# Both score parts of a pair's first head ahead of the transposed units, in the attentions of groups three and four

## The chip, the cores and the metric

One core of a Trainium2 chip runs the whole program. The metric is device time in microseconds (us); of several runs the median is taken. Five engines matter: TensorE (PE in the rows; PEld is its weight load), VectorE (DVE), ScalarE (ACT), GpSimd (POOL) and the DMA queue of SyncE (SP). Each runs its own instructions in program order and waits on semaphores for the others.

## What is computed

One layer of a decoder block over 2048 rows of 1024 columns: a projection, a convolution branch and a sparse attention branch, a gated merge with an output projection, a feed-forward part, and norms. The change touches only the attention, cut here to what matters:

```python
def block(xs):                       # one block of 128 queries
    start, qb, qib, wb = xs
    ...
    _, idx = lax.top_k(score, topk)  # 256 keys of each query
    ...
    att = jnp.einsum('bqhd,bqkd->bhqk', qb, k_sel) * (HEAD_DIM ** -0.5)
    att = att - slopes[None, :, None, None] * dist[:, None]
    p = jax.nn.softmax(att, axis=-1)
    return jnp.einsum('bhqk,bqkd->bqhd', p, v_sel)   # 8 heads, one shared key and value
```

The kernel does not gather the 256 keys. It computes the scores of every key up to the query's own block, adds a mask M that holds the distance and shuts out the keys that were not picked, and takes the softmax over the whole row.

## The kernel before

The rows are worked on in four groups of 512 (g = 0 to 3 in the code, groups one to four here). A group passes through a projection phase, an attention phase "C" and a feed-forward phase; the phases of different groups follow each other on TensorE. `halved(g)` is true in groups three and four, where a query row has up to 1536 and 2048 keys.

An attention of a group has 16 **pairs** of heads, `i` = 0 to 15: four query blocks of 128 rows, in each four pairs. In a pair, `e` is 0 for the first head and 1 for the second. The row of scores of a head has two **parts** in groups three and four: the first of 1024 keys, the second of what is left, 128, 256, 384 and 512 keys in the four blocks of group three, and 640, 768, 896 and 1024 in those of group four. Four engines work on it:

- TensorE computes a part's scores (L2086, L2087: four matmuls of 512 columns, or two to four narrower ones) into one of two score banks, which alternate. A part waits until the part two before it has been masked (`s_masked`).
- VectorE masks a part (L1667: one operation that reads the bank, adds M, keeps the least value and writes `probs`; a short second instruction reads the accumulator). The second part of a head starts from the first one's least value, so it waits for it.
- ScalarE takes the exponential of a head in two instructions (L1028), one for the first half of the row's tiles and one for the second.
- TensorE transposes the probabilities of the **preceding** pair in **units** of two tiles and two heads (L2033, four matmuls of 128 columns) into banks 4 and 5, which alternate from unit to unit. ScalarE copies a unit out as its high part (L1048), VectorE then writes the low part (L1675), and TensorE multiplies both by the values (L2055, L2056) two units later. One matmul at L2063 spreads the reciprocal sums.

A unit waits for two things: the exponentials of its tiles (`exp_done`), and the low part of the unit two before it (`pt_ready`), whose bank it takes. The units of the preceding pair's first tiles (three in group three, four in group four) belong to `e` = 0, and those of its last tiles to `e` = 1. `woven(g, i, e, lag, at)` deals them out over the parts; TensorE (L2074) and VectorE (L1658) both walk its list, so that both have the same order:

```python
for v, ks in woven(g, i, e, lag, at):
    ...  # score part v (TensorE), or its mask (VectorE)
    for k in ks:
        transposes(k)
        values(k - 2)
```

ScalarE's own loop (L1039 on) goes by `at` and does not call `woven`: the high copies of a head's units, between them the second exponential of the head before, and then the first exponential of this head, once its last part is masked.

In what follows the first, second, third and fourth unit of `e` = 0 are called U0, U1, U2 and U3 (U3 stands in `e` = 1 in group three), and the first and second score part P0 and P1.

Of the kernel before, what the change touches and what calls it, by code (L numbers as in the profile page):

```python
# [23 lines left out]
def build_block(nc, A):  # L24
# [166 lines left out]
    with ctx:  # L191
# [160 lines left out]
        def woven(g, i, e, lag, at):  # L352

            n = parts_of(g) if i < PAIRS else 0
            ks = at[i - lag, e] if i >= lag else range(0)
            if n == 0:
                return [(None, ks)]
            cut = [len(ks) * v // n for v in range(n + 1)]
            return [(v, ks[cut[v]:cut[v + 1]]) for v in range(n)]

        PT_BASE = [sum(len(slots(a)[0]) for a in range(g)) for g in range(GROUPS)]

        def parts_of(g):

            return (g + 2) // 2
# [19 lines left out]
        def halved(g):  # L385

            return g >= 2
# [803 lines left out]
        def _(dve):  # L1191
# [144 lines left out]
            for ph, g in ORDER:  # L1336
# [284 lines left out]
                elif ph == "C":  # L1621
# [18 lines left out]
                    for i in range(PAIRS + lag):  # L1640
# [4 lines left out]
                        for e in range(2):  # L1645
# [12 lines left out]
                            for v, ks in woven(g, i, e, lag, at):  # L1658
                                if v is not None:
                                    s, w = part_span(b, v)  # L1660
                                    r = part(g, i, e, v)
                                    last = v + 1 == parts_of(g)
                                    dve.wait_ge(s_psum, r + 1)
                                    if v:
                                        dve.wait_ge(s_masked, r)
                                    out = top if last else first_top[:, e:e + 1]
                                    nc.vector.tensor_tensor_reduce(out=prob(g, i, e)[:, s:s + w], in0=score_bank(r)[:, 0:w],  # L1667
                                                                   in1=M[:, b % RT % 2, s:s + w].bitcast(f32), scale=-2.0 ** -(h + 1),
                                                                   scalar=low, op0=ALU.add, op1=ALU.min, accum_out=out).then_inc(s_masked, 1)
                                    low = out  # L1670
                                for k in ks:

                                    w = table[k][2] * 2 * P
                                    dve.wait_ge(pt_hi, PT_BASE[g] + k + 1)
                                    nc.vector.tensor_tensor(out=pt_hl(g, k, len(table), 1, w), in0=PS[:, 4 + k % 2, 0:w],  # L1675
                                                            in1=pt_hl(g, k, len(table), 0, w).bitcast(f32), op=ALU.subtract).then_inc(pt_ready, 1)
                                    if marking and step < MARKS:
                                        mark(t, RT * g + t, u_mark, step)
                                        step += 1
                                    weigh(k - 3)  # L1680
# [83 lines left out]
        def _(pe):  # L1764
# [116 lines left out]
            for ph, g in ORDER:  # L1881
# [132 lines left out]
                elif ph == "C":  # L2014
# [50 lines left out]
                    for i in range(PAIRS + lag):  # L2065
                        for e in range(2):
                            if i < PAIRS:
                                t, h = i // (HEADS // 2), 2 * (i % (HEADS // 2)) + e
                                if g > 0 and t == 0 and e == 0:
                                    pe.wait_ge(qs_in[h // 2] if h else qs_first, 16 * g)  # L2070
                                elif g > 0 and t == 1 and h == 0:
                                    pe.wait_ge(qs_in[0], 16 * g)
                                lhs = QS[:, h, t * P:(t + 1) * P]
                            for v, ks in woven(g, i, e, lag, at):  # L2074
                                if v is not None:
                                    r = part(g, i, e, v)
                                    s0, w0 = part_span(RT * g + t, v)
                                    if r >= PART_BASE[g] + 2:
                                        pe.wait_ge(s_masked, r - 1)
                                    elif g > 0:  # L2080

                                        pe.wait_ge(ny_done, RT * (g - 1) + r - PART_BASE[g] + 1)
                                    for at_s in range(0, w0, 512):
                                        s, w = s0 + at_s, min(512, w0 - at_s)
                                        o = score_bank(r)[:, at_s:at_s + w]
                                        mm(o, lhs, KH[:, s:s + w], start=True, stop=False)  # L2086
                                        ins = mm(o, lhs, KL[:, s:s + w], start=False, stop=True)  # L2087
                                    ins.then_inc(s_psum, 1)
# [3 lines that stand above are left out]
# [65 lines left out]
```

## Time and profile before

| | |
|---|---|
| runs | 3293.29 us median of three (3289.09 to 3296.37) |
| profiled execution, span | 3293.2 us |
| TensorE busy | 3180.6 us (97%) |
| VectorE, ScalarE, GpSimd busy | 2023.7 (61%), 1300.5 (39%), 790.1 us (24%) |
| attention of group three, 1795 to 1942 us | TensorE busy 130.65 of 147 us, VectorE 117.00, ScalarE 120.09 |
| attention of group four, 2656 to 2845 us | TensorE busy 174.44 of 189 us, VectorE 149.38, ScalarE 150.47 |

The span is the time from the first to the last instruction of one execution. A busy time is a sum over the engine's instructions. In the two attentions VectorE and ScalarE have four fifths of the time filled, against 61% and 39% over the whole program.

### The profile page before, as it was taken

The numbers are of one execution on the slowest core, as the hardware profiler recorded it, in microseconds if no ns is written. First come the engines' busy times: TensorE is split into PE (matmuls) and PEld (weight loads), VectorE is DVE, ScalarE is ACT, GpSimd is POOL, SyncE is SP. The second block draws the span as 40 slices with busy tenths as digits, with TensorE's granted clock in tenths as the row PEclk, the third lists the DMA queues.
The fourth block names the chain that finished last, engine by engine and source line by source line (L and its number), as shares of the span: only waits on it lengthen the run. The fifth ranks groups of instructions, "written<-read, shape, count | busy, mean of one in ns | idle before, by whom it ended". The sixth has DMA issues, their size and how long they took to land.

```text
span 3293.2 us, 41912 instructions
## 1 busy us (share of the span) xinstructions
PE 3180.6 (97%) x15077; PEld 2620.5 (80%) x15077; DVE 2023.7 (61%) x3433; ACT 1300.5 (39%) x2213; POOL 790.1 (24%) x674
## 2 busy tenths in 40 slices
PE   8987999999999999999999999999999999999998
PEld 7865788788888888778887878876888888788886
DVE  6997357688807447599895862759667588510001
ACT  4336421533237431351112854228675168420111
POOL 3432200065775100011313520000212325101212
PEclk9998999999999999999999999999999999999999
DMA  7973856599893656535555046552555520445554
GB/s 236 302 242 128 307 188 208 185 292 289 290 298 122 243 202 216 195 139 194 192 192 185 14 182 226 206 180 90 217 192 193 201 74 20 173 166 193 194 196 165
DMA packets 178529, 635.97 MB, mean 193 GB/s; under 512 B 11358, under 2 KB 96906, under 8 KB 116777
## 3 DMA queue, kind: packets, MB, share of 16 engines
q1 hardware_dynamic: 164016, 583.05, 51.0%
q10 hardware_dynamic: 14328, 50.42, 3.9%
q8 instruction: 121, 1.98, 0.2%
q14 instruction: 64, 0.52, 0.0%
HBM read 474.04 MB, written 159.38 MB: 192 GB/s over the span
## 4 chain that ended last, share of the span: by engine, by line
PE 78%; ACT 5%; issue 3%; DVE 3%; DMA 1%; POOL 0%; ACTq 0%; DVEq 0%; POOLq 0%; SPq 0%
PE PS L1862 19%; PE PS L1813 15%; PE PS L1815 15%; PE PS L1814 15%; PE PS L2033 3%; PE PS L1836 2%; PE PS L1837 1%; PE PS L1838 1%; ACT TMP L903 1%; PE PS L2055 1%; PE PS L2056 1%; ACT probs L1028 1%; DVE W L1405 1%; PE PS L2086 1%; PE PS L2087 1%
## 5 line engine op out<-in xcount | busy, mean ns | idle before, releaser
L1862 PE MATMUL PS<-WS,HT 128*128 128x512 f32 x2088 | 482.7, 391 | 3.3 <-POOL WS L571 3.3
L1862 PEld LDWEIGHTS PS<-WS,HT 128*128 128x128 f32 x2088 | 393.9, 189 | 85.8 <-issue 3.7
L704 POOL TENSOR_TENSOR TMP<-TMP 128x512 f32<-128x512 f32 x88 | 114.5, 1302 | 1294.6 <-ACT TMP L1153 1294.6
L571 POOL TENSOR_TENSOR WS<-RAW,WS 128x1024 fp32r<-128x1024 f32 x116 | 279.9, 2413 | 569.1 <-ACT WS L776 556.3
L1813 PE MATMUL PS<-HF,WS 128*128 128x512 f32 x1024 | 398.7, 389 | 1.3 <-ACT TMP L903 0.9
L1815 PE MATMUL PS<-HF,WS 128*128 128x512 f32 x1024 | 398.4, 389 | 0.0
L1814 PE MATMUL PS<-HF,WS 128*128 128x512 f32 x1024 | 398.4, 389 | 0.0
L1422 DVE TENSOR_SCALAR_CACHE_REDUCE flags<-W,cand 128x640 uint8<-128x640 f32 (+9 forms) x272 | 372.6, 1370 | 35.6 <-DVE cand L1457 27.8
L1813 PE MATMUL PS<-HT,WS 128*128 128x512 f32 x816 | 322.2, 395 | 0.3 <-DVE HT L1242 0.3
L1815 PE MATMUL PS<-HT,WS 128*128 128x512 f32 x816 | 317.8, 389 | 0.0
L1814 PE MATMUL PS<-HT,WS 128*128 128x512 f32 x816 | 317.5, 389 | 0.0
L776 ACT ACTIVATE WS<-RAW 128x1024 fp32r<-128x1024 f32 x114 | 120.7, 1059 | 329.7 <-PE PS L1815 118.5
L1753 DVE TENSOR_TENSOR attn<-PS,XR 128x1024 f32<-128x1024 f32 x16 | 19.1, 1220 | 364.5 <-PE PS L1862 364.1
L1322 DVE SCALAR_TENSOR_TENSOR PS<-W,cw,PS 128x512 f32<-128x512 f32 x344 | 227.2, 744 | 0.0
L1813 PEld LDWEIGHTS PS<-HF,WS 128*128 128x128 f32 x1024 | 192.2, 188 | 42.1 <-ACT TMP L903 1.3
L1814 PEld LDWEIGHTS PS<-HF,WS 128*128 128x128 f32 x1024 | 192.2, 188 | 40.0
L1815 PEld LDWEIGHTS PS<-HF,WS 128*128 128x128 f32 x1024 | 192.2, 188 | 39.9
L2033 PE MATMUL PS<-ident,probs 128*128 128x128 f32 x1088 | 173.0, 280 | 25.1 <-ACT probs L1028 15.4
L1862 PE MATMUL PS<-W,HT 128*128 128x512 f32 x792 | 185.2, 389 | 0.0
L903 ACT ACTIVATE TMP<-PS 128x512 f32<-128x512 f32 (+3 forms) x304 | 155.7, 546 | 67.0 <-PE PS L1913 44.7
L1813 PEld LDWEIGHTS PS<-HT,WS 128*128 128x128 f32 x816 | 153.2, 188 | 34.5 <-issue 2.5
L1814 PEld LDWEIGHTS PS<-HT,WS 128*128 128x128 f32 x816 | 153.2, 188 | 33.0 <-issue 1.9
(287 smaller groups left out, 6417.0 us busy)
## 6 DMA issues: line engine op xcount, KB each, us to landing
WS<-split_weights_scratch SPq DMA_DIRECT2D x234, 1024.0 KB, 4.8
split_weights_scratch<-WS SPq DMA_DIRECT2D x116, 1024.0 KB, 5.0
W<-split_weights_scratch SPq DMA_DIRECT2D x114, 1024.0 KB, 4.8
RAW<-in_w_in SPq DMA_DIRECT2D x34, 512.0 KB, 6.1
RAW<-in_w_ffn_gate SPq DMA_DIRECT2D x22, 512.0 KB, 6.3
RAW<-in_w_ffn_up SPq DMA_DIRECT2D x22, 512.0 KB, 6.4
RAW<-in_w_ffn_down SPq DMA_DIRECT2D x22, 512.0 KB, 5.7
gate_b_scratch<-TMP ACTq DMA_DIRECT2D x32, 256.0 KB, 5.3
```

Of the source, the lines that this page charges most:

```text
L571: nc.gpsimd.tensor_tensor(out=WS[:, slot, 1, :], in0=RAW[:, slot, :], in1=WS[:, slot, 0, :].bitcast(f32), op=ALU.subtract).then_inc(w_lo, 1)
L704: nc.gpsimd.tensor_tensor(out=TMP[:, s, :], in0=TMP[:, s, :], in1=TMP[:, 2 + s, :], op=ALU.mult).then_inc(h_prod, 1)
L776: nc.scalar.activation(WS[:, slot, 0, :], RAW[:, slot, :], ACT.Copy).then_inc(w_hi, 1)
L903: nc.scalar.activation(TMP[:, idx_done % 4, 0:w], PS[:, idx_bank(g, n), 0:w], ACT.Relu, scale=DH ** -0.5).then_inc(idx_relu, 1)
L1322: nc.vector.scalar_tensor_tensor(out=TAPSUM[:, c, :], in0=GLU[:, c, ds(k0 + i, ROWS)], scalar=cw[:, c, ds(k0 + i, 1)], in1=TAPSUM[:, c, :] ...
L1422: step(nc.vector.tensor_scalar(flags[:, 0:n], keys(g, t, 0, n), cand[:, t:t + 1].bitcast(f32), 0.0, op, ALU.add, accum_out=count[:, t:t + 1]))
L1813: mm(PS[:, bank, :], wh, src[:, 0, k, :], start=k == 0, stop=False)
L1814: mm(PS[:, bank, :], wh, src[:, 1, k, :], start=False, stop=False)
L1815: ins = mm(PS[:, bank, :], wl, src[:, 0, k, :], start=False, stop=k == KD - 1)
L1836: mm(o, split(c, 0)[:, at], src(0, k), start=k == 0, stop=False)
L1862: ins = mm(PS[:, 2 * t + half, :], lhs, split(c, w_part)[:, half * 512:(half + 1) * 512], start=first and part == 0 and w_part == 0, stop= ...
L2033: ins = nc.tensor.transpose(PS[:, 4 + k % 2, (2 * a + e) * P:(2 * a + e + 1) * P], prob(g, i, e)[:, (k0 + a) * P:(k0 + a + 1) * P], ident[ ...
```

## The change

Where a group is halved, all units that belong to a pair's first head come behind its second part. Before, they were dealt out over both parts: in group three one unit behind P0 and two behind P1, in group four two and two. The second head keeps its order, and so do groups one and two, which have one part a head.

```diff
@@ -356,6 +356,8 @@
             if n == 0:
                 return [(None, ks)]
             cut = [len(ks) * v // n for v in range(n + 1)]
+            if halved(g) and e == 0:
+                cut[1:n] = [0] * (n - 1)
             return [(v, ks[cut[v]:cut[v + 1]]) for v in range(n)]
```

TensorE in group three, first head of pair 10: P0 of 1024 keys, U0 with the values of an older unit, P1 of 384 keys, and U1. Before:

```order
L2086 MATMUL PS<-KH,QS 128x512 [waits scores_masked]
L2087 MATMUL PS<-KL,QS 128x512
L2086 MATMUL PS<-KH,QS 128x512
L2087 MATMUL PS<-KL,QS 128x512
L2033 MATMUL PS<-ident,probs 128x128 [waits pt_ready,exp_done]
L2033 MATMUL PS<-ident,probs 128x128 x3
L2055 MATMUL PS<-PT,VV 128x256 [waits pt_ready]
L2056 MATMUL PS<-PT,VV 128x256
L2055 MATMUL PS<-PT,VV 128x256
L2056 MATMUL PS<-PT,VV 128x256
L2086 MATMUL PS<-KH,QS 128x384 [waits scores_masked]
L2087 MATMUL PS<-KL,QS 128x384
```

With the change (every line number is two higher):

```order
L2088 MATMUL PS<-KH,QS 128x512 [waits scores_masked]
L2089 MATMUL PS<-KL,QS 128x512
L2088 MATMUL PS<-KH,QS 128x512
L2089 MATMUL PS<-KL,QS 128x512
L2088 MATMUL PS<-KH,QS 128x384 [waits scores_masked]
L2089 MATMUL PS<-KL,QS 128x384
L2035 MATMUL PS<-ident,probs 128x128 [waits pt_ready,exp_done]
L2035 MATMUL PS<-ident,probs 128x128 x3
L2057 MATMUL PS<-PT,VV 128x256 [waits pt_ready]
L2058 MATMUL PS<-PT,VV 128x256
L2057 MATMUL PS<-PT,VV 128x256
L2058 MATMUL PS<-PT,VV 128x256
```

The two matmuls of P1 have moved ahead of U0 and of the four value matmuls behind it.

VectorE in group four, first head of pair 15: the mask of P0 (it writes `first_top`), the low parts of units, and the mask of P1 of 1024 keys (it reads `first_top`). Before:

```order
L1667 ISA probs,first_top<-PS,QI 128x1024 [waits s_psum,pt_psum]
L1667 ISA first_top 128x1
L1675 TENSOR_TENSOR PT<-PS,PT 128x512 [waits pt_hi] x2
L1667 ISA probs,mx<-PS,QI,first_top 128x1024 [waits scores_masked,s_psum]
L1667 ISA mx 128x1
L1675 TENSOR_TENSOR W<-PS,W 128x512 [waits pt_hi] x2
L1694 RECIPROCAL rs<-rs 128x2 [waits sums_of_halves_added]
```

With the change:

```order
L1669 ISA probs,first_top<-PS,QI 128x1024 [waits s_psum,pt_psum]
L1669 ISA first_top 128x1
L1669 ISA probs,mx<-PS,QI,first_top 128x1024 [waits scores_masked,s_psum]
L1669 ISA mx 128x1
L1677 TENSOR_TENSOR PT<-PS,PT 128x512 [waits pt_hi] x2
L1677 TENSOR_TENSOR W<-PS,W 128x512 [waits pt_hi] x2
L1696 RECIPROCAL rs<-rs 128x2 [waits sums_of_halves_added]
```

The mask of P1 has moved ahead of the low parts of U0 and U1, and stands directly behind the mask of P0.

## Rows read from the trace of the kernel before

**Rows 1.** The page, part 4: the chain that ended last, by engine.

```profile
PE 78%; ACT 5%; issue 3%; DVE 3%; DMA 1%; POOL 0%; ACTq 0%; DVEq 0%; POOLq 0%; SPq 0%
```

**Rows 2.** Waits, total us, times, longest: 1795 to 1942 us, then 2656 to 2845.

```profile
PE PS L2033 <- ACT probs L1028: 8.8, 14, 1.1
...
PE PS L2033 <- ACT probs L1028: 6.6, 15, 1.3
```

**Rows 3.** Timeline, group four, pair 15, first head: start, duration, engine, operation, idle before.

```profile
2815.06 0.40 PE L2086 MATMUL PS<-KH,QS 128*128 128x512 f32 x1
...
2815.29 0.40 PE L2087 MATMUL PS<-KL,QS 128*128 128x512 f32 x1
...
2816.56 0.66 PE L2033 MATMUL PS<-ident,probs 128*128 128x128 f32 x4 [0.41 <-ACT probs L1028]
2816.97 0.36 PE L2055 MATMUL PS<-W,VV 128*128 128x256 f32 x1
...
2819.60 0.60 PE L2033 MATMUL PS<-ident,probs 128*128 128x128 f32 x4
2819.95 0.36 PE L2055 MATMUL PS<-PT,VV 128*128 128x256 f32 x1
2820.11 1.27 DVE L1667 CUSTOM_DVE_ANT_0 probs<-PS,QI,first_top 128x1024 f32<-128x1024 f32 x1
...
2821.31 0.69 DVE L1675 TENSOR_TENSOR W<-PS,W 128x512 fp32r<-128x512 f32 x1
```

**Rows 4.** Timeline, group three, pair 10, first head.

```profile
1873.68 0.40 PE L2086 MATMUL PS<-KH,QS 128*128 128x512 f32 x1
...
1874.76 0.66 PE L2033 MATMUL PS<-ident,probs 128*128 128x128 f32 x4
1874.92 1.23 DVE L1667 CUSTOM_DVE_ANT_0 probs<-PS,QI 128x1024 f32<-128x1024 f32 x1 [0.49 <-PE PS L2087]
...
1876.08 0.69 DVE L1675 TENSOR_TENSOR W<-PS,W 128x512 fp32r<-128x512 f32 x1
...
1876.97 0.60 PE L2033 MATMUL PS<-ident,probs 128*128 128x128 f32 x4
```

**Rows 5.** Timeline, VectorE, group four, pair 0: masks of P0 and P1.

```profile
2656.28 1.21 DVE L1667 CUSTOM_DVE_ANT_0 probs<-PS,QI 128x1024 f32<-128x1024 f32 x1
...
2657.64 0.88 DVE L1667 CUSTOM_DVE_ANT_0 probs<-PS,QI,first_top 128x640 f32<-128x640 f32 x1
```

**Rows 6.** Groups by form, group four, then group three: busy us, mean ns, idle.

```profile
L1667 DVE CUSTOM_DVE_ANT_0 probs<-PS,QI,first_top 128x1024 f32<-128x1024 f32 x8 | 10.2, 1275 | 0.0
...
L1667 DVE CUSTOM_DVE_ANT_0 probs<-PS,QI,first_top 128x128 f32<-128x128 f32 x8 | 2.8, 344 | 0.3
```

**Rows 7.** Timeline, group three, pair 2, first head.

```profile
1808.20 0.40 PE L2086 MATMUL PS<-KH,QS 128*128 128x512 f32 x1
...
1809.82 0.66 PE L2033 MATMUL PS<-ident,probs 128*128 128x128 f32 x4 [0.54 <-ACT probs L1028]
...
1811.14 0.69 DVE L1675 TENSOR_TENSOR PT<-PS,PT 128x512 fp32r<-128x512 f32 x1 [0.49 <-ACT PT L1048]
...
1811.98 0.41 PE L2033 MATMUL PS<-ident,probs 128*128 128x128 f32 x2
```

**Rows 8.** Timeline, group three, pair 6, first head: U0 and U2.

```profile
1841.46 0.66 PE L2033 MATMUL PS<-ident,probs 128*128 128x128 f32 x4 [0.78 <-ACT probs L1028]
...
1843.80 0.60 PE L2033 MATMUL PS<-ident,probs 128*128 128x128 f32 x4
```

**Rows 9.** Timeline, P0 and U2 of group three's last and group four's first such pair.

```profile
1917.10 0.40 PE L2086 MATMUL PS<-KH,QS 128*128 128x512 f32 x1
...
1920.96 0.60 PE L2033 MATMUL PS<-ident,probs 128*128 128x128 f32 x4
...
2672.27 0.40 PE L2086 MATMUL PS<-KH,QS 128*128 128x512 f32 x1
...
2676.07 0.62 PE L2033 MATMUL PS<-ident,probs 128*128 128x128 f32 x4
```

## Prediction

> **What bounds the kernel now.** I read the page's chain first, then the waits and the timeline of the two attentions. TensorE makes up 78% of the chain that ended last, ScalarE 5%, VectorE 3% [rows 1]: whatever makes TensorE wait inside an attention lengthens the program one for one, since the phases follow each other on TensorE. The waits tell what there is to win. TensorE's transposes stood still for ScalarE's exponential for 8.8 us in group three (14 times) and 6.6 us in group four (15 times) [rows 2], about once a pair. The timeline shows where: in pair 15 of group four TensorE has sent off P0 and sits idle 0.41 us until the exponential that U0 needs is done [rows 3]. The change puts P1 into this gap. What it takes away is VectorE's early turn at U0's low part.
>
> **The measure.** I count each pair from the start of its P0 to the start of U2. Behind U2 the order on all engines is the old one, so I take what follows to move with it. U2 has two conditions. TensorE must have reached it, and the low part of U0 must be written, since both use the same bank. Between the start of a low part and a unit that waited for it alone lie 0.84 us: pair 2 of group three, 1811.14 to 1811.98 [rows 7].
>
> **Where U2 is now.** The start of P0 to that of U2 is 1811.98 - 1808.20 = 3.78 us in pair 2 of group three and 1920.96 - 1917.10 = 3.86 in pair 15; 2676.07 - 2672.27 = 3.80 in pair 2 of group four and 2819.60 - 2815.06 = 4.54 in pair 15 [rows 3, 7, 9]. Read the same way, the 14 pairs from 2 to 15 give 3.78, 4.16, 4.17, 4.26, 4.22, 4.23, 4.32, 4.36, 3.29, 3.29, 3.40, 3.42, 3.87, 3.86 in group three, and 3.80, 3.81, 3.87, 3.97, 4.31, 4.33, 4.44, 4.44, 4.22, 4.23, 4.33, 4.46, 4.54, 4.54 in group four.
>
> **Where VectorE will be.** It masks P0 from 1.24 us behind the start of P0 on (1874.92 - 1873.68, [rows 4]). P1's mask needs P0's least value. The trace has the two masks back to back only in pair 0, where the second starts 2657.64 - 2656.28 = 1.36 us behind the first [rows 5]; I take that for all pairs. P1's mask holds VectorE for its duration less 0.07 us, since a 1.27 us mask at 2820.11 is followed by a low part at 2821.31 [rows 3]. By width that is 0.27 us for 128 keys and 1.20 for 1024 [rows 6], on a line between them 0.13 more for every 128 keys. So U0's low part starts no earlier than 1.24 + 1.36 + m, and U2 no earlier than 3.44 + m, with m the mask's step: 3.71, 3.84, 3.98 and 4.11 in the four blocks of group three, 4.25, 4.38, 4.51 and 4.64 in those of group four. Now the low part of U0 starts at 2.40 us in pair 10 (1876.08 - 1873.68 [rows 4]).
>
> The other bound on U0's low part is ScalarE's high part: it starts 1.32 us behind U0 (1811.14 - 1809.82 [rows 7]), hence U2 at U0 + 2.16. This holds only where U0 itself is late, in pairs 2 to 9 of group three, where ScalarE's exponentials come last.
>
> **The sum, pair by pair.**
> - Group three, pairs 2 to 5: U2 already stands at U0 + 2.16 (1811.98 - 1809.82 [rows 7]), and U0 waits for ScalarE whatever TensorE does. P1's mask fits in VectorE's idle time. 0.
> - Pairs 6 to 9: U2 stands at U0 + 2.34 (1843.80 - 1841.46 [rows 8]) in two of them and 2.45 in the other two, because P1 lies between; it can fall to 2.16. The gain is 0.18, 0.18, 0.29 and 0.30: -0.95.
> - Pairs 10 to 13: no wait for the exponential now (U0 at 1.08 [rows 4]), so P1's move covers nothing. U2 goes from 3.29, 3.29, 3.40, 3.42 to 3.98, 3.98, 4.11, 4.11: +2.8.
> - Pairs 14 and 15: 3.87, 3.86 to 4.11: +0.5.
> - Group four, pairs 2 to 5, 6 to 9, 10 to 13, 14 and 15: 4.25, 4.38, 4.51, 4.64 less the times above: +1.8, +0.3, +1.1, +0.2, together +3.4.
> - Pair 1 of each group: TensorE is not up to speed and the queues are still short; P1 ahead of U0 delays U0 by about 0.3 us in group three, and in group four fills a longer gap by as much. 0, give or take 0.5.
>
> That is +5.8 us. One term more: a unit behind a wait is slower at the start. In pair 15 the values follow 0.41 us behind U0, which waited, and 0.35 behind U2, which did not [rows 3]. U2 waits newly in 24 pairs: +1.3. The whole is **+7.1 us**, against the profiled execution's 3293.2 us 3300.3; the median of the runs, 3293.29, is the same time, so it stays **3300.3 us**.
>
> What I cost at nothing: P1's scores are the same matmuls, and their bank is free, since the part two before was masked before P0 began. U0 comes later by P1's length (0.12 to 0.93 us), less the wait that it fills. That delays U0's and U1's high parts on ScalarE; for U1's low part and so for the unit behind U2 it is about a tie in pairs 14 and 15 of group four, and if it isn't, each pair pays up to 0.3 us again. ScalarE's and GpSimd's loops and all DMA queues keep their order.
>
> **A rule weighed.** The step of 1.36 us between the masks holds a wait of VectorE on its own semaphore. Before a low part, which has no such wait, it is 1876.08 - 1874.92 = 1.16 us [rows 4], so the trace charges 0.20 for it. The Trainium skill, "VectorE: DVE Perf Modes", section on the DRAIN, says that a semaphore between VectorE operations costs nothing extra. By that rule the masks would follow each other at the plain step. This case's trace speaks against it in pair 0, with the 0.20 us just named.
>
> **The rivals.**
> 1. The forecast, VectorE's mask of P1 decides U2: +5.5 to +9 us. Chance 0.47.
> 2. Part of the delay is taken up again. In pairs 10 to 13 of group three TensorE has no gap, but if ScalarE or VectorE then sets the pace behind U2, the delay there costs half, 7.1 - 1.4 = 5.7, and with the same in the first block of group four, 5.7 - 0.9 = 4.8: +3 to +5.5 us, about 3297.5. For it: the two engines are busy 0.8 of the attention. Against: behind U2 the timeline shows hardly a stop of TensorE. Chance 0.20.
> 3. The masks follow each other at VectorE's plain step of 1.16 us. Then U2 is 0.20 us earlier in the 24 pairs that it decides, -4.8, and the total is +2.3 us, 3295.6. Against it is the only place that shows the step. Chance 0.15.
> 4. Faster: U0's low part is in time, and the filled gap is a gain. A part of 1024 keys takes four matmuls 0.23 us apart (2815.29 - 2815.06 [rows 3]), 0.93 us. In pair 15 of group four U0 would start behind two of them at 1.86 us instead of 1.50, and without P1 in between U2 would follow at 4.54 + 0.36 - 0.93, about 3.95, instead of 4.54, -0.6; some -0.5 in 14 pairs of group four and -0.2 in ten of group three: -9 us, 3284. It decides where U0's low part starts before about 3.05 us; the two masks alone end at 3.40 and more in group four. Chance 0.06.
> 5. Worse: U1's low part is late as well, because U0 is, and the unit behind U2 waits again. 0.3 us in 24 pairs on top: +14 us, 3307. For it the tie named above. Chance 0.12.
>
> **How the numbers follow.** A measurement of this kernel tells 0.2%, 6.6 us, from no change. The forecast sits at that edge: of its 0.47 I count 0.35 above it and 0.12 below. Slower by over 0.2%: 0.35 + 0.12 = 0.47. Within: 0.12 + 0.20 + 0.15 = 0.47. Faster: 0.06. The range reaches from 3291.5, which takes in rivals 2 and 3 with the runs' own spread of some 3 us, to 3307. The forecast's own range is 3298.8 to 3302.3.
>
> **What would show it.** In the changed trace TensorE's wait for the exponential should nearly vanish in group four and in the last blocks of group three, and a wait for VectorE's low part should stand before U2, some 0.5 to 0.9 us in the pairs of group four. The two masks should start 1.36 us apart in every first head. P0 to U2 should read 3.98 in pair 10 of group three and 4.64 in pair 15 of group four. The attention of group four should be 3 to 5 us longer, that of group three 2 to 4, and everything outside them unchanged. The prediction is wrong if the step between masks is 1.16, if U2 doesn't wait for VectorE, or if the part behind U2 gets shorter as U2 comes later.

## The result and the profile after the change

The changed kernel took 3302.68 us, the median of ten runs (3300.7 to 3304.85); the kernel before, on the same chip, 3294.64 us, also ten (3289.09 to 3297.58). The ratio is 1.0023, with a 95% interval of 1.0014 to 1.0032: slower by 7.6 us. (This ratio and those below are estimated from all runs; they are not the quotient of the two medians, which differ by 8.0 us here.) The forecast was 7.1 us slower.

The page of the changed kernel: its span, the busy times, and the chain that ended last.

```profile
span 3300.0 us, 41912 instructions
...
PE 3179.3 (96%) x15077; PEld 2623.3 (79%) x15077; DVE 2026.4 (61%) x3433; ACT 1300.3 (39%) x2213; POOL 795.5 (24%) x674
...
PE 76%; ACT 5%; DVE 5%; issue 3%; POOL 0%; DMA 0%; ACTq 0%; DVEq 0%; POOLq 0%; SPq 0%
```

The busy times are those of before to within 6 us on every engine: no work was added. In the chain TensorE lost two points and VectorE won two, against [rows 1]. The profiled execution took 3302.19 us, of which 3300.0 are the span, 6.8 more than before.

What TensorE's transposes waited for, in group three's attention (first three rows) and in group four's (last three): total us, times, longest.

```profile
PE PS L2035 <- ACT probs L1030: 6.0, 12, 1.1
...
PE PS L2035 <- DVE PT L1677: 3.0, 4, 0.9
PE PS L2035 <- DVE W L1677: 2.3, 4, 0.8
...
PE PS L2035 <- DVE PT L1677: 8.1, 14, 0.8
...
PE PS L2035 <- DVE W L1677: 2.4, 4, 0.7
PE PS L2035 <- ACT probs L1030: 2.4, 2, 1.3
```

Set beside [rows 2]: in group four the wait for the exponential fell from 6.6 to 2.4 us, and of its two cases one stands in pair 1 and the other behind the last head, so that none is left in pairs 2 to 15. In its place stand 10.5 us of waiting for VectorE's low parts (L1677), 9.6 of them before U2 in pairs 2 to 15. Before it was 1.0 us:

```profile
PE PS L2033 <- DVE PT L1675: 1.0, 4, 0.5
```

One wait was traded for a longer one.

The timeline of group three's pair 10, and behind the "..." that of group four's pair 15: start, duration, engine, operation, idle before.

```profile
1873.86 0.40 PE L2088 MATMUL PS<-KH,QS 128*128 128x512 f32 x1
...
1875.08 1.23 DVE L1669 CUSTOM_DVE_ANT_0 probs<-PS,QI 128x1024 f32<-128x1024 f32 x1 [0.46 <-PE PS L2089]
1875.12 0.60 PE L2035 MATMUL PS<-ident,probs 128*128 128x128 f32 x4
...
1876.46 0.62 DVE L1669 CUSTOM_DVE_ANT_0 probs<-PS,QI,first_top 128x384 f32<-128x384 f32 x1
...
1877.00 1.37 DVE L1677 TENSOR_TENSOR W<-PS,W 128x512 fp32r<-128x512 f32 x2
...
1877.83 0.63 PE L2035 MATMUL PS<-ident,probs 128*128 128x128 f32 x4 [0.73 <-DVE W L1677]
...
2821.77 0.39 PE L2088 MATMUL PS<-KH,QS 128*128 128x512 f32 x1
...
2822.99 1.23 DVE L1669 CUSTOM_DVE_ANT_0 probs<-PS,QI 128x1024 f32<-128x1024 f32 x1
...
2823.62 0.60 PE L2035 MATMUL PS<-ident,probs 128*128 128x128 f32 x4
...
2824.36 1.28 DVE L1669 CUSTOM_DVE_ANT_0 probs<-PS,QI,first_top 128x1024 f32<-128x1024 f32 x1
...
2825.57 0.69 DVE L1677 TENSOR_TENSOR PT<-PS,PT 128x512 fp32r<-128x512 f32 x1
...
2826.41 0.63 PE L2035 MATMUL PS<-ident,probs 128*128 128x128 f32 x4 [0.58 <-DVE PT L1677]
2826.50 0.69 DVE L1677 TENSOR_TENSOR PT<-PS,PT 128x512 fp32r<-128x512 f32 x1 [0.24 <-ACT PT L1050]
2826.79 0.36 PE L2057 MATMUL PS<-PT,VV 128*128 128x256 f32 x1
...
2827.35 0.62 PE L2035 MATMUL PS<-ident,probs 128*128 128x128 f32 x4
```

Read each part from the top: P0, its mask on VectorE, U0, the mask of P1, the low part of U0, and U2, which waited for it. In pair 15 U0 no longer waits (in [rows 3] it did, 0.41 us). U2 does: it stands 2826.41 - 2821.77 = 4.64 us behind P0, where it stood at 4.54. In pair 10 it is 1877.83 - 1873.86 = 3.97, and was 1876.97 - 1873.68 = 3.29 [rows 4]. The rows behind U2 in pair 15 show the next unit 0.94 us later, 0.85 behind the start of U1's low part at 2826.50.

Per attention I compare the stretch from the start of pair 2's P0 to the last matmul that spreads the sums (L2063 before, L2065 after). In group three it grew from 127.71 to 130.77 us, in group four from 167.18 to 170.87. Together that is 6.75 us of the span's 6.8.

### The profile page after: what moved, and what is told of

Its sections match the earlier page's. It is cut to its first block, busy times and chain, and to the rows that moved or that the text cites. A ratio compares the mean times of both kernels' runs of the same rounds, so it can differ in the third digit from the quotient of the medians.

```text
span 3300.0 us, 41912 instructions
## 1 busy us (share of the span) xinstructions
PE 3179.3 (96%) x15077; PEld 2623.3 (79%) x15077; DVE 2026.4 (61%) x3433; ACT 1300.3 (39%) x2213; POOL 795.5 (24%) x674
## 4 chain that ended last, share of the span: by engine, by line
PE 76%; ACT 5%; DVE 5%; issue 3%; POOL 0%; DMA 0%; ACTq 0%; DVEq 0%; POOLq 0%; SPq 0%
PE PS L1864 19%; PE PS L1815 15%; PE PS L1817 15%; PE PS L1816 15%; PE PS L2035 2%; DVE probs L1669 2%; PE PS L1838 1%; ACT TMP L905 1%; PE PS L1839 1%; PE PS L1840 1%; PE PS L2057 1%; PE PS L2058 1%; DVE W L1407 1%; PE PS L2088 1%; PE PS L2089 1%
## 5 line engine op out<-in xcount | busy, mean ns | idle before, releaser
L1864 PE MATMUL PS<-WS,HT 128*128 128x512 f32 x2088 | 481.8, 390 | 4.3 <-POOL WS L573 4.3
L1864 PEld LDWEIGHTS PS<-WS,HT 128*128 128x128 f32 x2088 | 392.9, 188 | 86.8 <-issue 5.1
L1864 PE MATMUL PS<-W,HT 128*128 128x512 f32 x792 | 185.2, 389 | 0.0
```

What stands on the lines that cost most here:

```text
L1864: ins = mm(PS[:, 2 * t + half, :], lhs, split(c, w_part)[:, half * 512:(half + 1) * 512], start=first and part == 0 and w_part == 0, stop= ...
```

## The experiments

The theory is the forecast's: in a first head VectorE now masks P1 before it writes U0's low part, and U2 waits for that. The rivals were that U1's low part or a late restart decides, that ScalarE paces the pair, or that TensorE's own order costs the time. Lengths of stretches are from pair 2's P0 to the last spread of sums, as above, each from one trace; the **period** of a pair is the time from its P0 to the next pair's. All medians are of 11 runs, but for the kernel with VectorE's order alone, with 4. Each is set against runs of the kernel before on the same chip. Where an interval reaches 1.0000 the time alone tells no difference, and the reading rests on the stretches.

**One group at a time.** The change in group three alone, and then in group four alone:

```diff
+            if g == 2 and e == 0:
+                cut[1:n] = [0] * (n - 1)
```
```diff
+            if g == 3 and e == 0:
+                cut[1:n] = [0] * (n - 1)
```

> The change in group three alone. If the cost is VectorE's mask of P1 ahead of U0's low part, pair by pair, the attention of group three is as in the changed kernel: P0 to U2 3.97 us in pair 10, the pairs 6 to 9 about 0.11 us shorter each, pairs 10 to 15 0.3 to 0.8 longer each, together +3.1 us, and the time is 3294.6 + 3.1 = 3297.7 us. The attention of group four keeps its old times, only 3 to 4 us later. If the loss were one of something that the two attentions share (a queue that stays late from one to the other), the two halves would not add up to the whole 8 us.

> The change in group four alone. VectorE's mask: the 14 pairs 2 to 15 are 0.07 to 0.56 us longer each, the first four and the fifth to the twelfth in turn as in the changed kernel, +3.7 us, with pair 1 some 0.5 us shorter: about 3297.8 us. Rival: the gain that the filled wait for the exponential promised shows here alone, some -5 us, 3290.

Measured: 3298.33 us against 3295.03 (ratio 1.0008, 0.9999 to 1.0017) and 3298.75 (1.0012, 1.0003 to 1.0021). In the traces the changed attention has the whole kernel's length to within 0.1 us, 130.70 in group three and 170.86 in group four, and the one left alone that of before, 127.68 and 167.18. The two costs add up, +3.0 and +3.7, and neither attention touches the other. The interval of the first kernel still takes in 1.

**One engine at a time.** `woven` got one more argument. In one kernel only TensorE passes `True`, so that VectorE keeps its old order; in the other only VectorE does.

```diff
-        def woven(g, i, e, lag, at):
+        def woven(g, i, e, lag, at, ahead):
...
+            if ahead and halved(g) and e == 0:
+                cut[1:n] = [0] * (n - 1)
```

> TensorE has the new order (P0, P1, then the units), VectorE the old one (the low parts of the first units ahead of P1's mask). My theory, that the loss is VectorE's order: U2 falls back to U0 + 2.16 us or to the time when TensorE reaches it: about 3.44 in pair 10 of group three (3.97 in the changed kernel), 3.56 in pairs 12 to 15, 4.0 in pair 15 of group four (4.64). The unit behind it, U3 in group four, then waits for U1's low part, because U0 came later by P1's length less the old wait: 0 to 0.25 us in each of 14 pairs. Sum about -1 in group three and +1.5 in group four: 3294 to 3297 us, 5 to 8 us below the changed kernel. Rival, that TensorE's own order costs: it stays near 3302 us. Rival, that only the wait for the exponential mattered: 3287 us or less.

> VectorE has the new order (both masks ahead of the low parts), TensorE the old one (P1 behind U0, in group four behind U0 and U1). My theory: U0's low part now waits for P1's scores and their mask. Group four: P1 is done 3.9 to 4.7 us behind P0's start, its mask 0.8 to 1.2 later, U2 0.84 behind that: +1.8 to +2.2 us in 14 pairs, +28. Group three: +0.3 to +0.8 in 14 pairs, +7. Together about 3329 us. If VectorE's order were harmless and TensorE's the cost, the time would be near 3294.6 us.

TensorE alone: 3295.41 us, ratio 1.0001 (0.9992 to 1.0010), and 126.59 and 167.07 us in the traces, -1.1 and -0.1. VectorE alone: 3335.53, ratio 1.0120 (1.0104 to 1.0135), and 135.23 and 197.80 us, +7.5 and +30.6; I had expected 3329. The waits of TensorE in this second kernel, in group four:

```profile
PE PS L2035 <- DVE PT L1677: 22.1, 13, 2.1
PE PS L2035 <- DVE W L1677: 7.0, 4, 1.8
PE PS L2035 <- ACT probs L1030: 6.6, 15, 1.3
```

The 6.6 us for the exponential are unchanged, and 29.1 us of waiting for VectorE stand beside them, where the kernel before had 1.0. This kernel loses more than the change does, because its mask of P1 also waits for scores that TensorE still sends behind the first units. The clean comparison is the changed kernel with TensorE's order alone: they differ in VectorE's order only, and it costs 4.2 us in group three and 3.8 in group four. TensorE's order by itself costs nothing. So the loss comes with VectorE's order. Why TensorE's alone gains so little in group four is in its timeline of pair 15:

```profile
2815.20 0.39 PE L2088 MATMUL PS<-KH,QS 128*128 128x512 f32 x1
...
2818.18 1.14 ACT L1030 ACTIVATE probs<-probs,mx 128x1024 f32<-128x1024 f32 x1
...
2819.15 0.63 PE L2035 MATMUL PS<-ident,probs 128*128 128x128 f32 x4
...
2819.31 0.59 ACT L1050 ACTIVATE PT<-PS 128x512 fp32r<-128x512 f32 x1
...
2819.94 0.69 DVE L1677 TENSOR_TENSOR PT<-PS,PT 128x512 fp32r<-128x512 f32 x1 [0.93 <-ACT PT L1050]
...
2820.77 0.63 PE L2035 MATMUL PS<-ident,probs 128*128 128x128 f32 x4 [0.53 <-DVE PT L1677]
```

U2 is early, 3.95 us behind P0 instead of 4.54. This is the value that the forecast's fourth rival gave for it. But the unit behind it waits for U1's low part, that one for its high part, and the high part stands on ScalarE behind an exponential of 1.14 us. It starts 5.57 us behind P0; before it was 5.45, 0.91 behind U2. The gain is gone one unit later.

**The chain between the masks cut.** The changed kernel, with P1's mask free of P0's least value. This leaves out part of the computation: the shift inside the softmax is then the least value of P1 and 0, not that of the whole row.

```diff
-                                    if v:
-                                        dve.wait_ge(s_masked, r)
...
-                                    low = out
+                                    low = 0.0
```

> The changed kernel, but P1's mask starts from the constant 0 instead of P0's least value and doesn't wait for P0's mask (so the shift of the softmax is the least of P1 and 0, not of the whole row; the output is another one). It measures the step between the two masks, which the forecast took as 1.36 us. My theory: 0.20 us of it is VectorE's wait on its own semaphore; the step falls to 1.16, P0 to U2 to 4.44 in pair 15 of group four, and 20 or more pairs are 0.20 us shorter: -4 to -5 us, 3298 us. By the Trainium skill, VectorE: DVE Perf Modes, on the DRAIN, the semaphore costs nothing extra and the step and the time stay at 1.36 and 3302.7 us.

Measured: 3295.29 us against 3294.37, ratio 1.0003 (0.9994 to 1.0012), and 128.17 and 167.28 us in the traces, 2.6 and 3.6 less than the changed kernel. I had expected 4 to 5 less in all. Pair 15 of group four, P0, VectorE and U2:

```profile
2811.47 0.40 PE L2086 MATMUL PS<-KH,QS 128*128 128x512 f32 x1
...
2812.70 1.22 DVE L1667 CUSTOM_DVE_ANT_0 probs<-PS,QI 128x1024 f32<-128x1024 f32 x1
...
2813.85 1.22 DVE L1667 CUSTOM_DVE_ANT_0 probs<-PS,QI 128x1024 f32<-128x1024 f32 x1
...
2815.00 0.69 DVE L1675 TENSOR_TENSOR PT<-PS,PT 128x512 fp32r<-128x512 f32 x1
...
2815.83 0.63 PE L2033 MATMUL PS<-ident,probs 128*128 128x128 f32 x4 [0.30 <-DVE PT L1675]
```

The step from mask to mask falls from 2824.36 - 2822.99 = 1.37 us to 1.15. P1's mask now holds VectorE 1.15 us instead of 2825.57 - 2824.36 = 1.21. Its start value is now a constant and no longer read from memory, as P0's always was, whose mask of the same width took 1.23 us where P1's took 1.28; this part I had not counted. Together 0.28 us a pair, and U2 moves by just that, from 4.64 to 2815.83 - 2811.47 = 4.36. In the 14 pairs of group four and in pairs 10 to 15 of group three it moves by 0.28 to 0.31, in pairs 8 and 9 of group three by 0.2, and in its pairs 2 to 7 by 0.1 or less. So VectorE's chain of masks decides U2 in 22 first heads, but not in the first ones of group three. The edit takes out the wait and the reading of the value together.

**ScalarE's order.** After the kernel with TensorE alone the exponential between the high parts was suspect. The second exponential of the head before is put behind the second high part instead of the first, in the kernel before and then with TensorE's new order:

```diff
-                                if u == 0:
+                                if u == (1 if halved(g) else 0):
                                     second_half(i, e)
```

> The kernel before, but ScalarE copies U1's high part ahead of the second exponential instead of behind it (groups three and four, both heads). U1's low part no longer waits for the exponential. In the kernel before U3 follows U2 by 0.92 us without a wait, so I expect next to nothing: 3293 to 3296 us. It is the partner of the next run.

> TensorE has the new order, VectorE the old one, and ScalarE copies U1's high part ahead of the second exponential. With TensorE's new order alone U3 stood still for U1's low part (1.62 us behind U2 instead of 0.92 in pair 15 of group four), which waits for that exponential. My theory: this is the second thing that eats the filled gap; with it gone U3 follows U2 by 0.95 us, and group four's 14 pairs are 0.1 to 0.55 us shorter than before, -5 us, group three's about -1: 3287 to 3291 us, and faster than both kernels. Rival: VectorE is then late with the second head's masks and the next pair's U0 waits again: 3293 to 3297 us.

Alone it gives 3299.74 us against 3294.37, ratio 1.0009 (1.0000 to 1.0018; its runs spread from 3292.95 to 3302.23, and the medians are 5.4 us apart), with 131.19 and 167.87 us in the traces: +3.5 in group three and +0.7 in group four, where I had expected nothing. U0 comes later there in pairs 6 to 9 (1.99 to 2.09 us behind P0 instead of 1.87 to 1.90), and the periods of pairs 10 to 14 grow by 0.25 to 0.5. With TensorE's new order it gives 3291.78 us, ratio 0.9994 (0.9985 to 1.0003), and 128.29 and 163.81: group four gains 3.4 us, group three loses 0.6. I had expected 3287 to 3291; by the time alone it is not told from the kernel before.

**What the pieces give together.** TensorE's order only in group three, but not in its third block; TensorE's order with the later exponential in the first heads of group four alone; and that same exponential in the changed kernel, whose VectorE has the new order:

```diff
+            if ahead and g == 2 and i // 4 != 2 and e == 0:
+                cut[1:n] = [0] * (n - 1)
```
```diff
-                                if u == 0:
+                                if u == (1 if g == 3 and e == 0 else 0):
```

> TensorE's new order in group three alone, without its third block (pairs 8 to 11), VectorE's order as before. Pairs 6 and 7 lose P1 between U0 and U2 (0.15 us each), pairs 14 and 15 gain about 0.3 each, pairs 12 and 13 lose 0.15 each: -0.5 us, no difference that can be measured; 3294 us.

> TensorE has the new order in both groups, VectorE the old one, and ScalarE copies U1's high part ahead of the second exponential only in first heads of group four. The run before this with the exponential late in both heads and both groups lost in group three (first exponentials later, U0 waits again) what it won in group four. My theory: group three now has the times of TensorE's new order alone (-1.1 us against the kernel before), and group four at least the gain of the later exponential, -3.4 us, likely -4 to -5 because the second heads get their exponential early again: 3289 to 3291 us. Rival: the second heads were not what held U0 up, and it stays at 3292 to 3293.

> The changed kernel, and ScalarE copies U1's high part ahead of the second exponential in first heads of group four. If VectorE's two masks are what holds U2, ScalarE's order can't help: P0 to U2 stays 4.64 us in pair 15 and the time stays 3301 to 3303 us. If the loss had come from U1's high part, it would fall to about 3298.

The first: 3297.37 us, ratio 1.0009 (1.0000 to 1.0018), though the stretch of group three is 0.75 us shorter and that of group four unchanged. In its trace pair 2 begins 2.6 us later than in that of the kernel before (1810.84 against 1808.20), of which more below. The second: 3292.88 against 3295.68, ratio 0.9989 (0.9980 to 0.9998), with 126.62 and 165.11 us, -1.1 and -2.1. It is the only kernel whose interval lies below 1, by 0.0002: a gain of some 0.1%, which the stretches bear out with 3.2 us. Its time is not in the 3289 to 3291 that I had expected but in what the rival gave, 3292 to 3293. The third: 3303.27, ratio 1.0019 (1.0010 to 1.0028), 130.71 and 171.01 us, as the change itself: while VectorE's masks decide U2, ScalarE's order is worth nothing.

The second kernel, first head of pair 14 of group four: P0, the high parts, the exponential, and the two units.

```profile
2800.74 0.39 PE L2088 MATMUL PS<-KH,QS 128*128 128x512 f32 x1
...
2804.14 0.60 ACT L1050 ACTIVATE PT<-PS 128x512 fp32r<-128x512 f32 x1 [0.31 <-PE PS L2035]
2804.63 1.14 ACT L1030 ACTIVATE probs<-probs,mx 128x1024 f32<-128x1024 f32 x1
2804.70 0.63 PE L2035 MATMUL PS<-ident,probs 128*128 128x128 f32 x4
...
2805.63 0.61 PE L2035 MATMUL PS<-ident,probs 128*128 128x128 f32 x4
```

U1's high part now stands ahead of the exponential, and the unit behind U2 follows it without a wait, 2805.63 - 2800.74 = 4.89 us behind P0, where TensorE's order alone had 5.57. Yet a pair's period is only 0.04 to 0.07 us shorter in pairs 9 to 14 than with TensorE's order alone, and 0.21 to 0.35 in pairs 2 to 8. In the last blocks the second heads gave back nearly all of it. The expected gain in group four, 4 to 5 us, came out as 2.1. The trace shows part of it: in the second heads of pairs 9 to 15 the last unit waits 0.21 to 0.31 us for the low part of the unit two before it, where with TensorE's order alone no second head of pairs 2 to 15 waits. The rest of the 0.5 to 0.6 us that these heads are longer I did not separate: with the exponential moved in both heads the periods of pairs 10 to 14 were 0.4 to 0.5 us shorter than here, and those of pairs 2 to 8 0.1 to 0.4 longer.

## Why the prediction was right

**The bound.** That what lengthens an attention lengthens the program one for one held: 6.75 us of attention, 6.8 of span, 7.6 of time. The median of 3302.68 us lies just above the forecast's own range, 3298.8 to 3302.3, because that range stood on 3293.29 for the kernel before, and ten runs gave 3294.64; the difference lies inside its +5.5 to +9.

**Where U2 stands.** The bound 3.44 + m was forecast as 4.25, 4.38, 4.51 and 4.64 us in the blocks of group four. Measured, the 14 pairs from 2 to 15: 4.24, 4.24, 4.40, 4.38, 4.38, 4.37, 4.54, 4.50, 4.51, 4.51, 4.66, 4.64, 4.64, 4.64. In pairs 10 to 15 of group three 3.98, 3.98 and four times 4.11 were forecast, and 3.97, 3.98, 4.15, 4.12, 4.12, 4.13 measured. The four terms are in the rows above: 1875.08 - 1873.86 = 1.22, 1876.46 - 1875.08 = 1.38, 1877.00 - 1876.46 = 0.54, 1877.83 - 1877.00 = 0.83.

**The sum.** U2's part was forecast at 5.8 us and came to 6.2, 2.8 in group three and 3.4 in group four. The difference is in pairs 6 to 9 of group three, whose gain was forecast at 0.95. U2 reached 4.07 and 4.08 in the first two, as it should, but 4.21 and 4.23 in the others instead of 4.03 and 4.06; the periods gained 0.44 in all. There VectorE decided already, where the forecast had ScalarE. In pair 8 it was still at an older low part when P0's scores were ready, so that its mask began 1.47 us behind P0 and not 1.24. The kernel before shows the same there, 1.46; the forecast had read the 1.24 in pair 10 and taken it for all pairs. The term for the slower restart was too large: forecast 1.3, and all that was lost behind U2 is 0.6. The values follow U2 by 2826.79 - 2826.41 = 0.38 us in pair 15 and by 0.39 in pair 10, against 0.35 unhindered, not by the 0.41 of a U0 that waited for ScalarE. Two terms were mis-sized, the first too low by 0.4 us and the second too high by 0.7. The mechanism was right; that the total came this near is partly luck. The stretches ahead of pair 2's P0, put at 0 give or take 0.5, came out 0.6 us longer in group three and 0.6 shorter in group four, which also cancels.

**The step of 1.36 between the masks.** It had one place in the trace to rest on, and it held: 1.37 and 1.38 in the two pairs shown, and U2 within 0.05 us of the bound 3.44 + m in each of the 20 pairs for which the forecast used it. (The third rival took 0.20 us off 24 pairs, -4.8; by the forecast's own sum it was these 20, -4.0.) The Trainium skill, "VectorE: DVE Perf Modes", section on the DRAIN, has a semaphore between VectorE operations cost nothing extra. By that rule the kernel with the chain cut should have kept its step; it fell to 1.15. So the third rival is out, and the measurement decides: what the page measured on copies does not hold here for an operation that waits for the one directly before and reads its result.

**The tie.** U1's low part was taken to be in time for the unit behind U2. In pair 15 it starts at 2826.50, and 0.84 us later is 2827.34; the unit stands at 2827.35, 0.94 behind U2, where an unhindered one stood 0.91 behind. A tie indeed, and the fifth rival is out for that reason alone: the cover was 0.03 us short, not 0.3.

**The rival that ended on the other side** was right in its sum for U2 (about 3.95; with VectorE's order kept 3.95), and wrong on two counts. With VectorE's new order U2 can't get there. And even there it brings next to nothing in group four, 0.1 us, since U1's low part is late by way of ScalarE. The prediction named that second stop for its own sum and in the fifth rival, but the fourth left it out: its 9 us would not have come even with U0's low part in time.

**What TensorE's order did.** The wait for the exponential vanished in group four as forecast, and in group three it stayed in pairs 2 to 9, where U0 waits for ScalarE whatever TensorE does.

## What to carry to other kernels

When an engine's gap is filled with work moved forward, look at who consumes that work, and what it now stands in front of there: here the gap was TensorE's, and the price was paid on VectorE, where P1's mask came ahead of an operation that frees a bank. A list that two engines share is worth splitting before it is changed, because the order that is good for the producer can be the wrong one for the consumer; TensorE's move without VectorE's cost nothing, and became a small gain only once ScalarE's order was made to fit as well. Follow a gain for at least two units past the wait that it removes: here U1's low part was nearly late already, and took the gain back.

## What the runs showed that was not expected

**A dependent operation on VectorE costs 0.2 us more.** With the wait for its predecessor's least value a mask starts 1.37 us behind it, without the wait and the value 1.15. The 0.22 us go with the wait and not with the reading as such: where P1's mask reads the value behind a low part, no idle time stands before it (0.0 us for the eight masks of 1024 keys in [rows 6]). With 0.06 us for each start value that is read, this made up 6.2 us of the two stretches.

**The first two pairs of an attention vary by more than the effects sought.** In group three of the changed kernel TensorE stands still for 2.51 us ahead of pair 0's second head and for 1.25 ahead of pair 1, and its clock is low for a while after. How long differed. The changed kernel and the one with group three changed alone are the same program up to the end of this attention, and both had these two stops. The stretch from pair 1's P0 to pair 2's, in the changed kernel and then in the other: length, busy us of PE, PEld, DVE, ACT and POOL, granted clock, DMA share, GB/s.

```profile
1800.41:1808.82 8.41, 7.46 (x42) 6.64 (x43) 5.69 (x13) 6.12 (x17) 5.28 (x9) 0.80 0.63 256
```
```profile
1798.19:1808.89 10.70, 10.05 (x42) 8.80 (x43) 6.11 (x14) 6.32 (x17) 5.24 (x9) 0.55 0.52 208
```

The same 42 matmul records took 7.46 us of TensorE at a granted clock of 0.80 and 10.05 us at 0.55: in the second trace more of the stretch passed at the lower of its two levels, 1.2 instead of 2.4 GHz. From the start of the last block of projection matmuls ahead of this attention (L1864, 144 matmuls; L1862 in the kernel before) to pair 2's P0 the two took 47.40 and 49.74 us; the kernel before took 47.12. That is why the lengths from pair 2 on, which repeat to 0.15 us, were used beside the ratios. Whether it also explains the medians that are 0.1% up where the attentions are not, as in the kernel with TensorE's order in group three's blocks, stays open, since there is one trace of each; and what decides how long the low level lasts was not tried.
